# A trunk of mLSTM, attention and product-key experts: part of the expert dots moved from VectorE to GpSimd and ScalarE

## The reference, cut to what matters

```
act = gelu(einsum('td,ted->te', x_blk, u[i_blk]))      # u: 16384 x 2048
out = einsum('te,ted->td', g_blk * act, v[i_blk])      # v: 16384 x 2048
```

## Time and profile before

| what | us |
|---|---|
| median of three runs | 3355.64 |
| the profiled execution, its own time | 3357.06 |
| its span, first to last instruction | 3355.3 |
| VectorE busy | 2600.2 |
| GpSimd busy | 1606.6 |
| ScalarE busy | 1269.1 |
| TensorE busy | 2093.6 |
| dot phase, layer 0 (438 to 1177) and layer 1 (2052 to 2790) | 739 and 738 |
| block 1's groups (1177 to 1250, 2790 to 2862) | 73 and 72 |
| value phase (1250 to 1750, 2862 to 3340) | 500 and 478 |

### The profile page before, as it was taken

How to read it: one execution, slowest core, us unless ns; L and a number is a source line. 1 busy time by engine, 2 the same in 40 slices (tenths; PEclk the granted TensorE clock), 3 DMA queues, 4 the chain that set the end, 5 groups by cost and what they waited for, 6 DMA issues and landing times.

```text
span 3355.3 us, 25410 instructions
## 1 busy us (share of the span) xinstructions
PE 2093.6 (62%) x7428; PEld 1389.1 (41%) x7428; DVE 2600.2 (77%) x3749; ACT 1269.1 (38%) x3645; POOL 1606.6 (48%) x1051
## 2 busy tenths in 40 slices
PE   7999964421330069999929998444032104999994
PEld 6887853320220054444418787333022104444441
DVE  4454589999999976655685758999999998666667
ACT  4444344445875570000003543444477647100000
POOL 1000065666666626654560004666665762566655
PEclk9999987765555579999969999666555556999997
DMA  6554689999989939999984448999998994899999
GB/s 231 180 186 138 228 356 419 419 386 388 346 310 355 402 106 402 409 407 408 408 312 152 137 138 344 420 417 391 385 347 313 363 382 169 323 409 409 409 408 357
DMA packets 247609, 1096.43 MB, mean 327 GB/s; under 512 B 23208, under 2 KB 23984, under 8 KB 176944
## 3 DMA queue, kind: packets, MB, share of 16 engines
q0 software_dynamic: 147456, 805.37, 60.7%
q1 hardware_dynamic: 96640, 282.22, 22.6%
q10 hardware_dynamic: 3376, 7.23, 0.6%
HBM read 1092.63 MB, written 2.11 MB: 326 GB/s over the span
## 4 chain that ended last, share of the span: by engine, by line
DVE 37%; DMA 27%; PE 19%; issue 8%; POOL 7%; ACT 2%; ACTq 0%; SPq 0%; DVEq 0%; POOLq 0%
DVE ring_sb L1888 23%; DMA actT_sb<-in_peer_vg_dram,idx_all 16%; PE bank L1041 15%; DMA ring_sb<-in_peer_vg_dram,idx_all 5%; DMA ring_sb<-in_peer_u_dram,idx_all 4%; DVE x_sb L1879 3%; POOL ring_sb L600 3%; POOL actT_sb L615 3%; DVE gain L1861 2%; PE bank L1306 1%; POOL ring_sb L615 1%; ACT gain L838 1%; DVE shared L1617 1%; DVE shared L1613 1%; DVE pair_all L1621 1%
## 5 line engine op out<-in xcount | busy, mean ns | idle before, releaser
L600 POOL DMA_INDIRECT ring_sb<-in_peer_u_dram,idx_all x496 | 917.2, 1849 | 504.1 <-DVE idx_all L1622 362.1
L1879 DVE SCALAR_TENSOR_TENSOR x_sb<-actT_sb,gate_rows,x_sb 128x1024 f32<-128x1024 f32 x340 | 434.6, 1284 | 234.2 <-DMA actT_sb<-in_peer_vg_dram,idx_all 227.7
L1888 DVE CUSTOM_DVE_ANT_0 ring_sb<-ring_sb,arena 128x2048 f32<-128x2048 f32 x256 | 572.9, 2287 | 23.9 <-DMA ring_sb<-in_peer_u_dram,idx_all 23.3
L615 POOL DMA_INDIRECT actT_sb<-in_peer_vg_dram,idx_all x340 | 421.9, 1241 | 352.6 <-DVE x_sb L1879 300.0
L1888 DVE CUSTOM_DVE_ANT_0 ring_sb<-ring_sb,actT_sb 128x2048 f32<-128x2048 f32 x256 | 573.0, 2287 | 0.0
L1041 PE MATMUL bank<-w_parts,actT_hi 128*128 128x512 f32 x1664 | 521.7, 395 | 7.1 <-DVE w_parts L416 5.0
L1319 PE MATMUL bank<-ring_sb,arena 128*128 128x512 f32 x1024 | 485.3, 596 | 6.4 <-DMA ring_sb<-in_peer_vd_dram 4.1
L1319 PE MATMUL bank<-ring_sb 128*128 128x512 f32 x1024 | 482.5, 594 | 0.0
L1306 PE MATMUL bank<-gain 128*128 128x128 f32 x1024 | 223.6, 392 | 341.1 <-DVE gain L1861 159.4
L416 DVE TENSOR_TENSOR w_parts<-ring_sb,w_parts 128x2048 fp32r<-128x2048 f32 x100 | 229.7, 2302 | 212.9 <-ACT w_parts L410 212.7
L1088 PE MATMUL bank<-arena 128*128 128x256 f32 x896 | 249.6, 445 | 209.4 <-DVE shared L1888 209.2
(11 more groups left out here) (199 smaller groups left out, 2431.6 us busy)
## 6 DMA issues: line engine op xcount, KB each, us to landing
ring_sb<-in_peer_vd_dram SPq DMA_DIRECT2D x128, 1024.0 KB
ring_sb<-in_mlstm_w_in_dram SPq DMA_DIRECT2D x48, 1024.0 KB, 5.1
arena<-in_peer_wq_dram SPq DMA_DIRECT2D x28, 1024.0 KB, 13.7
ring_sb<-in_attn_w_in_dram SPq DMA_DIRECT2D x20, 1024.0 KB, 5.1
ring_sb<-in_mlstm_w_out_dram SPq DMA_DIRECT2D x16, 1024.0 KB, 5.0
ring_sb<-in_attn_w_out_dram SPq DMA_DIRECT2D x16, 1024.0 KB, 5.0
ring_sb<-in_peer_u_dram,idx_all POOLq DMA_INDIRECT x496, 10.7
actT_sb<-in_peer_vg_dram,idx_all POOLq DMA_INDIRECT x340
```

The lines of the kernel that those rows point to most:

```text
L600: nc.gpsimd.indirect_dma_start(out=ring[i % NU], out_offset=None, in_=u_tab[l], in_offset=bass.IndirectOffsetOnAxis(ap=rows_at, axis=0),). ...
L615: nc.gpsimd.indirect_dma_start(out=g_slot[j % NG], out_offset=None, in_=vg_tab[l], in_offset=bass.IndirectOffsetOnAxis(ap=idx_all[b][:, p: ...
L1879: v.scalar_tensor_tensor(out=xb[b][:, DENSE:D], in0=g_slot[j % NG], scalar=w_all[b][:, p:p + 1], in1=xb[b][:, DENSE:D], op0=ALU.mult, op1= ...
L1888: v.tensor_tensor_reduce(ring[i % NU], ring[i % NU], rows[b], 1.0, 0.0, ALU.mult, ALU.add, dots[u % 2][:, k:k + 1]).then_inc(dot_done, 1)
```

## The change

Three parts.

First, of every unit but unit 0, dots k = 4 and k = 11 (`POOL_K`, `pooled`) leave VectorE: 30 of 256 per layer. GpSimd multiplies the ring slot by the tokens' rows in place (`product`, one `tensor_tensor` 128x2048), behind the gather that is eight later (`PRODUCT_BEHIND`). ScalarE then sums the slot by a Copy with an accumulator over 2048, ahead of its five small instructions. Waits on a dot go to `dot_done` or `dot_summed`, as the dot is (`wait_dot`).

Second, the one-hot and weighted tiles have four slots in block 1 (`DEPTH`), two in `gain` and two over `rows_1`. ScalarE writes one-hot groups 1 and 3 ahead of block 1's groups and then runs four ahead. VectorE waits for all products before the first of these groups.

Third, since `rows_1` is in use for longer, the first twelve gathers of `v` go over four slots. The two slots over `rows_1` are first used by gathers 16 and 17, after block 1's last group.

```diff
+        POOL_K = (4, 11)
+        def pooled(i):
+            return i >= TOPK and i % TOPK in POOL_K
+        def wait_dot(eng, l, i):
+            if pooled(i):
+                eng.wait_ge(dot_summed, l * POOL_DOTS + pool_dots(i))
+            else:
+                eng.wait_ge(dot_done, l * DVE_DOTS + dve_dots(i))
...
+            PRODUCT_BEHIND = 8
+            def product(l, i):
+                b = i // (HEADS * TOPK)
+                pool.wait_ge(xn_ready, 2 * (2 * l + 1) + b + 1)
+                pool.wait_ge(u_landed[i % NU], 16 * uses(i, l, NU, LAYER_TILES))
+                nc.gpsimd.tensor_tensor(ring[i % NU], ring[i % NU], rows_1 if b else xn[0],
+                                        ALU.mult).then_inc(product_ready, 1)
...
                         if i >= NU:
-                            pool.wait_ge(dot_done, l * LAYER_TILES + i - NU + 1)
+                            wait_dot(pool, l, i - NU)
                         nc.gpsimd.indirect_dma_start(
                             out=ring[i % NU], out_offset=None, in_=u_tab[l],
                             in_offset=bass.IndirectOffsetOnAxis(ap=rows_at, axis=0),
                         ).then_inc(u_landed[i % NU], 16)
+                        if pooled(i - PRODUCT_BEHIND):
+                            product(l, i - PRODUCT_BEHIND)
...
-                        act.wait_ge(dot_done, gu * TOPK + k + 1)
+                        if pooled(i):
+                            act.wait_ge(product_ready, l * POOL_DOTS + pool_dots(i))
+                            nc.scalar.activation(ring[i % NU], ring[i % NU], ACT.Copy,
+                                                 accum_out=d[:, c]).then_inc(dot_summed, 1)
+                        wait_dot(act, l, i)
...
                     for k in range(TOPK):
-                        expert(k)
+                        if not pooled(u * TOPK + k):
+                            expert(k)
...
-        onehot_2 = [gain[:, i * CH:(i + 1) * CH].rearrange("p (t e) -> p t e", e=P) for i in range(2)]
-        weighted_1 = [gain[:, (2 + i) * CH:(3 + i) * CH].rearrange("p (t e) -> p t e", e=P) for i in range(2)]
+        spread = [gain[:, i * CH:(i + 1) * CH].rearrange("p (t e) -> p t e", e=P) for i in range(4)]
+        spread += [rows_1[:, i * CH:(i + 1) * CH].rearrange("p (t e) -> p t e", e=P) for i in range(4)]
+        onehot_2, weighted_1 = spread[0::2], spread[1::2]
+        DEPTH = [2, 4]
...
+        G_EARLY = 12
+        G_SLOT = [j % 4 if j < G_EARLY else (j - G_EARLY) % NG for j in range(NB * PICKS)]
...
+                if j == G_EARLY + 4:
+                    pool.wait_ge(wb_full, (2 * l + 2) * GROUPS)
+                if G_BEFORE[j] >= 0:
+                    pool.wait_ge(vg_added, l * NB * PICKS + G_BEFORE[j] + 1)
...
                 onehot_group(1, 1)
+                onehot_group(1, 3)
                 for g in range(GROUPS):
                     weights_group(1, g)
-                    if g % 2 and g + 2 < GROUPS:
-                        onehot_group(1, g + 2)
+                    if g % 2 and g + 4 < GROUPS:
+                        onehot_group(1, g + 4)
```

More of the change, by code:

```diff
@@ L315, in trunk_kernel, with value_landed, pool_dots, dve_dots @@
         G_ORDER = [(j % NB, j // NB) for j in range(NB * PICKS)]
-        D_PAIRS = P // 2
+        G_EARLY = 12
+        G_SLOT = [j % 4 if j < G_EARLY else (j - G_EARLY) % NG for j in range(NB * PICKS)]
+        G_USE = [G_SLOT[:j].count(G_SLOT[j]) for j in range(NB * PICKS)]
+        G_BEFORE = [max([-1] + [i for i in range(j) if G_SLOT[i] == G_SLOT[j]]) for j in range(NB * PICKS)]
+        def value_landed(l, j):
+            return 16 * (l * G_SLOT.count(G_SLOT[j]) + G_USE[j] + 1)
+        D_PAIRS = P // 2
+        POOL_K = (4, 11)
+        def pooled(i):
+            return i >= TOPK and i % TOPK in POOL_K
+        def pool_dots(i):
+            return sum(pooled(t) for t in range(i + 1))
+        def dve_dots(i):
+            return i + 1 - pool_dots(i)
+        POOL_DOTS, DVE_DOTS = pool_dots(LAYER_TILES - 1), dve_dots(LAYER_TILES - 1)
+        def wait_dot(eng, l, i):
[3 more added lines that the diff above has]
+                eng.wait_ge(dot_done, l * DVE_DOTS + dve_dots(i))
         def uses(i, l, slots, per_layer):
@@ L500, in load_dense @@
                     if p < ND:
-                        sp.wait_ge(dot_done, l * LAYER_TILES + LAYER_TILES - 8 + p + 1)
+                        wait_dot(sp, l, LAYER_TILES - 8 + p)
                     else:
@@ L609, in values @@
                 elif j < 4:
[L610 to L614, removed]
+                    wait_dot(pool, l, LAYER_TILES - NU + 7)
+                if j == G_EARLY + 4:
+                    pool.wait_ge(wb_full, (2 * l + 2) * GROUPS)
+                if G_BEFORE[j] >= 0:
+                    pool.wait_ge(vg_added, l * NB * PICKS + G_BEFORE[j] + 1)
                 nc.gpsimd.indirect_dma_start(
-                    out=g_slot[j % NG], out_offset=None, in_=vg_tab[l],
+                    out=g_slot[G_SLOT[j]], out_offset=None, in_=vg_tab[l],
                     in_offset=bass.IndirectOffsetOnAxis(ap=idx_all[b][:, p:p + 1], axis=0),
-                ).then_inc(vg_landed[j % NG], 16)
+                ).then_inc(vg_landed[G_SLOT[j]], 16)
             def experts(l):
                 gathers(l)
+                for i in range(LAYER_TILES - PRODUCT_BEHIND, LAYER_TILES):
+                    if pooled(i):
+                        product(l, i)
                 for j in range(NB * PICKS):
@@ L828, in onehot_group @@
                 def onehot_group(b, g):
[L830 to L833, removed]
+                    wait_spread(act, l, b, g)
+                    if g < 2:
                         at = GR[f"t{l}"] + b
                         act.wait_ge(tr_out[at % 2], at // 2 + 1)
+                    rows = onehot_2[g % DEPTH[b]]
                     for j in range(GROUP):
                         t = GROUP * g + j
-                        st.did(nc.scalar.activation(onehot_2[g % 2][:, j, :], numbers, ACT.Abs,
+                        st.did(nc.scalar.activation(rows[:, j, :], numbers, ACT.Abs,
                                                     bias=picks_T[:, P + t:P + t + 1], scale=-1.0))
                     st.need(st.n)
-                    nc.scalar.activation(onehot_2[g % 2], onehot_2[g % 2], ACT.Relu, bias=1.0,
+                    nc.scalar.activation(rows, rows, ACT.Relu, bias=1.0,
                                          scale=-1.0).then_inc(onehot_act, 1)
@@ L1854, in weighted_group @@
                 def weighted_group(b, g):
-                    at = (2 * l + b) * GROUPS + g
-                    if at >= 2:
-                        dve.wait_ge(wb_full, at - 1)
+                    wait_spread(dve, l, b, g)
                     for j in range(GROUP):
                         t = GROUP * g + j
-                        last = v.tensor_scalar(weighted_1[g % 2][:, j, :], numbers, picks_T[:, t:t + 1],
+                        last = v.tensor_scalar(weighted_1[g % DEPTH[b]][:, j, :], numbers, picks_T[:, t:t + 1],
                                                picks_T[:, 2 * P + t:2 * P + t + 1], ALU.is_equal, ALU.mult)
@@ L1864, in weighted_group @@
                     if b == 1 and g % 2 == 0:
-                        v.tensor_tensor(onehot_2[0], numbers.unsqueeze(1).to_broadcast([P, GROUP, P]),
+                        v.tensor_tensor(onehot_2[g % DEPTH[b]], numbers.unsqueeze(1).to_broadcast([P, GROUP, P]),
                                         picks_T[:, P + GROUP * g:P + GROUP * (g + 1)].unsqueeze(2).to_broadcast([P, GROUP, P]),
@@ L1878, in add_value @@
                         dve.wait_ge(weight_done, (l + 1) * LAYER_TILES)
-                    v.scalar_tensor_tensor(out=xb[b][:, DENSE:D], in0=g_slot[j % NG], scalar=w_all[b][:, p:p + 1],
+                    v.scalar_tensor_tensor(out=xb[b][:, DENSE:D], in0=g_slot[G_SLOT[j]], scalar=w_all[b][:, p:p + 1],
                                            in1=xb[b][:, DENSE:D], op0=ALU.mult, op1=ALU.add).then_inc(vg_added, 1)
@@ L1915, in peer @@
                 wait_groups(dve, GR[f"t{l}"] + 1, 1)
+                dve.wait_ge(product_ready, (l + 1) * POOL_DOTS)
                 for g in range(GROUPS):
```

14 lines of the change are left out of this document (11 added, 3 removed).

## The result

The changed kernel takes 3459.25 us (median of four, 3454.99 to 3465.23) against 3355.19 us before: ratio 1.031 (95% interval 1.029 to 1.033), 104 us slower. The forecast was 3461. Its profiled execution has a span of 3458.4 us, 103.1 more than before.

What follows compares the result with a forecast made beforehand. VectorE was taken to bound the dot phases, with the DMA close behind. From the profiled 3357.1 us, +114 (dot phases), -16 (block 1's groups) and +6 (V gathers) gave +104, to 3461; range for 8 in 10: 3375 to 3560.

Steps and rivals of the forecast that it cites:

- VectorE sets the dot phase, the DMA is close behind: Layer 0's dot phase: VectorE sets its 739 us; with VectorE free, DMA would let it lose at most about 60 us.
- A product takes 4.4 us: One 128x2048 product on GpSimd: 0.2 us fixed plus 4 x 1.05; the ends kept were 3.3 and 5.0 us.
- Product and two-input instruction take turns: A GpSimd product waits up to one dot, then holds VectorE's next two-input instruction for its full 4.4 us.
- The size of the holds: VectorE's stall in dot phases: 4.4 us per product 11; product 4 leaves 1.5 in block 0, 2.5 in units 12 to 14.
- Late gathers: Block 0 units: gathers issued later make VectorE wait 2 to 9 us, taken as 4, with about 1 absorbed.
- Four slots: Block 1's groups: one-hot rows further ahead remove most of ScalarE's wait for TensorE; -8 us per layer (0 to -10).
- ScalarE's own 63 us are the bound: Block 1's groups: once most of its wait goes, ScalarE's work of 33.3 + 19.3 + 10.1 = 62.7 us sets the length.
- Twelve gathers over four slots: Value phase: two V gathers missing by the groups' end, 1 MB, move in the full DMA; +3 us per layer.
- Rival A: Products run beside the dots without stopping VectorE; units 6 to 15 save 44 us per layer, to 3259; chance 0.12.
- Rival B: Product takes 3.3 us, largely on the router's steps, gathers land in time; 3374 us, range 3350 to 3395, chance 0.12.
- Rival C: ScalarE or the landing decides: landing wait 9 us and ScalarE's lag shows; 3580 us, from 3550 on, chance 0.10.

Runs made afterwards that it cites:

- the slots alone: Against the kernel before: all 256 dots stay on VectorE, four slots and the twelve gathers over four slots are kept; 3329.97 us, ratio 0.993.

## Why the prediction was right

*VectorE sets the dot phase, the DMA is close behind.* Right. Without products the phase ended 39 us earlier, with the DMA at 0.99.

*A product takes 4.4 us.* 4.50 free, 5.74 with the rest of a dot in front. Right. The 1.25 us rows of 128x512 gave it with a fixed part of 0.2 us, which was an assumption; 4.50 for four times the work leaves 0.17.

*Product and two-input instruction take turns.* Right, and it was the deciding step. It rested on two overlaps at the kernel's start and on gathers ending 0.88 us behind dots. The run with rows in PSUM shows it: same products, no dot held, 138 us less. The tensor_scalar of block 0's groups, of which no row before could tell, was held too (22 us per layer); the 3.5 us per unit that the prediction took there left it little shelter.

*The size of the holds.* The terms were 15 x 4.4 = 66 us for product 11 and 36 us for product 4, 102 us per layer; measured 119 in both layers. Product 11 was right (4.36 each when alone). Product 4 was taken as half sheltered (1.5 us left in block 0); alone it held VectorE for 3.2 us. The shelter ends at L1645, the first two-input step behind 3 us of one-input ones, and this I hadn't counted as a hold; and with product 11 ahead of it, it left more of the product over. Under-sized by 17 us per layer.

*Late gathers.* The term was 7 x (4 - 1) = 21 us per layer, measured +10 and +6. It was over-sized by 11 to 15 us: the prediction named 9.7 us as the lower landing time, and the landing in question took 9.5. The mechanism is real: in four pieces it made 38 us more in layer 0.

So the dot phase was forecast as +57 per layer and came out as +67 and +63.

*Four slots.* Forecast -8, measured -11.6 and -13.1. The step that was off is "ScalarE's own 63 us are the bound": the 62.7 us were a sum of lines whose instructions overlap, and the earlier trace rows has ScalarE busy for 60.8 us in this stretch. By line, block 1's groups after (busy, mean ns | idle before), against the earlier trace rows:

```profile
L902 ACT COPY ring_sb<-bank 128x512 f32<-128x512 f32 x32 | 30.8, 1056 | 1.1 <-PE bank L1365 1.1
L1919 DVE TENSOR_SCALAR gain<-const,shared 128x128 f32<-128x128 f32 x64 | 19.0, 357 | 2.9 <-ACT shared L398 2.9
```

ScalarE's wait for TensorE went from 10.5 to 1.1 us, and two copies in a row now overlap (1.92 us for both, 1.04 for one before), so its busy time also shrank: 58 us in a phase of 61.5.

*Twelve gathers over four slots.* Forecast +3, measured -1.3 and -3.0 in the value phase. With the slots alone it was +1.2 and -1.4. The two missing gathers can't be told from other shifts; the term is not confirmed.

The total (+104 forecast, +103.1 in the profile) is closer than its parts: dots 8 us per layer too low, groups and values 9 us per layer too high. That these cancel to 1 us is luck. Rival A was the other real candidate; the run without products shows what it would have meant, 3250 us. Rival B took 3.3 us for a product, where 4.50 was measured. Rival C's ScalarE part didn't show: ScalarE waited for a product for up to 12.4 us, but VectorE's waits for ScalarE were 1.0 and 2.5 us per dot phase. With four pieces they were 12 and 14 us.

## What to carry to other kernels

Before moving work from VectorE to GpSimd, look at what VectorE runs meanwhile: count its instructions with two SBUF inputs, and its tensor_scalar, copies and casts. Here a GpSimd product over SBUF stood as a stop of nearly its own length for whichever of them it met (4.0 of 4.5 us on average). If one operand of the hot VectorE instruction is reused, try it in PSUM: here that cost at most 9 us of copies, and 60 products that had cost 129 us then gained 6 us (3327 to 3321), or 24 us (3327 to 3303) with 40 of them placed clear of the tensor_scalar. Then look at what the freed time runs into; here the DMA gave back only 39 of 66 us per layer.

## What the runs showed of the hardware that was not expected

A memset on GpSimd, which reads nothing, holds a 128x128 tensor_scalar of VectorE (0.34 us, then up to 2.5), a 128x32 cast now and then, and no two-input dot (2344 ns at most). A product cut in four pieces costs as much hold as one piece (4 x 1.05 us) and made GpSimd wait for dots, 12.3 us for the four pieces. A dot over four PSUM banks and SBUF has the same 2286 ns (median) as one over two SBUF operands (2281 and 2285).
